# Half of the output projection computed inside the attention stage, and the prompt's compressed attention placed in its first steps

## What is computed

```python
q, g, cmp_r, sel_r, win_r, u = project(xp, norm1_g[l], w_in[l], ...)
o, win_state = nsa_prompt(q, g, cmp_r, sel_r, win_r, ...)      # sample: nsa_sample
y_pool, pool_state = pool_mix(u, ...)
...
def finish(x, o_attn, y_pool, w_out, norm2_g, peer_wq, ...):
    mix = jnp.concatenate([o_attn.reshape(B, T, ATTN_WIDTH), y_pool], axis=-1)
    h = x + jnp.einsum('btc,cd->btd', mix, w_out)
    return h + peer_ffn(rmsnorm(h, norm2_g), peer_wq, ...)
```

## Time and profile before

| | us |
|---|---|
| median of three runs | 1728.66 (1724.99 to 1734.77) |
| the profiled execution's own time | 1730.21 |
| its span | 1728.5 |
| `attend`, first matmul to the end of the last, in the trace | 146.3 to 351.5 |
| output projection, eight tiles | 353.8 to 404.6 |

### The profile page before, as it was taken

One profiled execution on the slowest core, in us unless ns is written; L12 is line 12 of the kernel. 1 busy time (PEld: TensorE's weight loads), 2 busy tenths in 40 slices (PEclk: granted clock), 3 DMA queues, 4 the chain that ended last, 5 costly groups with the idle time before them and its releaser, 6 DMA issues.

```text
span 1728.5 us, 29474 instructions
## 1 busy us (share of the span) xinstructions
PE 1669.6 (97%) x10320; PEld 1577.6 (91%) x10320; DVE 1368.2 (79%) x2811; ACT 736.4 (43%) x1391; POOL 495.2 (29%) x454
## 2 busy tenths in 40 slices
PE   8998998899998999999999999989999999999999
PEld 6876765589998999999999999989999999999999
DVE  3273457654788999999998998856998999999996
ACT  1121355443223334665666668833333333333332
POOL 0003232011000233333322244332443454444440
PEclk9999988899999999999999999989999999999999
DMA  7527242123222798888898999998999999999994
GB/s 223 185 62 219 74 122 76 38 86 99 78 68 92 259 320 306 292 317 310 305 319 305 314 327 373 377 346 282 373 390 377 365 396 393 391 395 398 393 394 143
DMA packets 188646, 457.31 MB, mean 265 GB/s; under 512 B 25858, under 2 KB 93954, under 8 KB 188034
## 3 DMA queue, kind: packets, MB, share of 16 engines
q1 hardware_dynamic: 111922, 245.27, 40.4%
q0 software_dynamic: 50416, 182.63, 28.8%
q10 hardware_dynamic: 26160, 27.53, 4.6%
HBM read 402.71 MB, written 56.05 MB: 265 GB/s over the span
## 4 chain that ended last, share of the span: by engine, by line
PE 61%; DVE 4%; DMA 2%; issue 1%; ACT 0%; SPq 0%; DVEq 0%; ACTq 0%
PE ps L1994 9%; PE ps L1997 9%; PE ps L2000 9%; PE ps L1970 9%; PE ps L1966 9%; PE ps L1967 9%; PE ps L2016 5%; DVE sb_w_lo L1799 1%; DMA gates_dense<-sb_g_stage 1%; DMA sb_ring<-expert_v 1%; DVE sb_slot L1836 0%; DMA sb_ring<-expert_u 0%; DVE sb_rows_y L1929 0%; DVE sb_hot L1835 0%; ACT sb_w_hi L1703 0%
## 5 line engine op out<-in xcount | busy, mean ns | idle before, releaser
L1703 ACT ACTIVATE sb_w_hi<-sb_ring 128x1024 fp32r<-128x1024 f32 x256 | 271.6, 1061 | 521.6 <-PE ps L2000 219.0
L1799 DVE TENSOR_TENSOR sb_w_lo<-sb_ring,sb_w_hi 128x1024 fp32r<-128x1024 f32 x256 | 313.0, 1223 | 74.8 <-ACT sb_w_hi L1703 68.2
L1966 PE MATMUL ps<-sb_x_hi,sb_w_hi 128*128 128x384 f32 x1024 | 353.4, 345 | 11.6 <-ACT sb_scores L1717 7.2
L1967 PE MATMUL ps<-sb_x_lo,sb_w_hi 128*128 128x384 f32 x1024 | 348.4, 340 | 0.0
L1970 PE MATMUL ps<-sb_x_hi,sb_w_lo 128*128 128x384 f32 x1024 | 202.6, 339 | 4.5 <-DVE sb_w_lo L1799 4.5
L1966 PEld LDWEIGHTS ps<-sb_x_hi,sb_w_hi 128*128 128x128 f32 x1024 | 194.4, 190 | 12.2 <-ACT sb_w_hi L1703 12.2
L1994 PE MATMUL ps<-sb_x_lo,sb_w_hi 128*128 128x384 f32 x1016 | 198.1, 336 | 5.4 <-ACT sb_x_lo L1712 5.3
L2000 PE MATMUL ps<-sb_x_lo,sb_w_hi 128*128 128x384 f32 x1016 | 197.6, 336 | 0.0
L1997 PE MATMUL ps<-sb_x_lo,sb_w_lo 128*128 128x384 f32 x1016 | 197.6, 336 | 0.0
L1967 PEld LDWEIGHTS ps<-sb_x_lo,sb_w_hi 128*128 128x128 f32 x1024 | 194.8, 190 | 0.0
L1693 POOL DMA_INDIRECT sb_scores<-expert_u_rows,sb_row_expert x80 | 103.5, 1293 | 307.2 <-DVE sb_row_dots L1918 216.0
(11 more groups left out here) (332 smaller groups left out, 2521.2 us busy)
## 6 DMA issues: line engine op xcount, KB each, us to landing
sb_ring<-expert_u SPq DMA_DIRECT2D x128, 512.0 KB
sb_ring<-expert_v SPq DMA_DIRECT2D x128, 512.0 KB
gates_dense<-sb_g_stage ACTq DMA_DIRECT2D x12, 2048.0 KB
hid_dense<-sb_hid SPq DMA_DIRECT2D x112, 192.0 KB
sb_scores<-hid_dense SPq DMA_DIRECT2D x112, 192.0 KB
sb_g_stage<-gates_dense SPq DMA_DIRECT2D x32, 384.0 KB
sb_g_stage<-gates_dense SPq DMA_DIRECT2D x48, 256.0 KB
sb_ring<-peer_wq SPq DMA_DIRECT2D x16, 512.0 KB
```

The source lines that it names most:

```text
L1703: nc.scalar.activation(whi[v % 2][:, :], ring(v)[:, :], ACT.Copy).then_inc(w_hi, 1)
L1799: nc.vector.tensor_tensor(wlo[v % 2][:, :], ring(v)[:, :], whi[v % 2][:, :], ALU.subtract).then_inc(w_lo, 1)
L1966: nc.tensor.matmul(out, hi[:, c * P:(c + 1) * P], g.x_hi[:, c], start=(c == 0), stop=False)
L1967: nc.tensor.matmul(out, hi[:, c * P:(c + 1) * P], g.x_lo[:, c], start=False, stop=False)
```

## The change

1. **Pooled half.** In steps 12 to 27, one piece n per step, PE computes the contribution of chunks 4 to 7 (pooling) to half n % 2 of the columns of output tile n // 2: four plain fp32 matmuls of 128x272 into bank 5 (`pooled`). DVE then adds the result to `g.xT` in place. Piece n waits until the add of piece n - 1 is made.
2. **Output projection.** `product` runs over four chunks instead of eight for the eight output tiles, so 24 matmuls instead of 48; high and low part are made of 512 columns of each `w_out` tile, and the split of `mixT` is of four chunks instead of eight. The query projection is unchanged.
3. **Compressed attention.** `cmp_scores` at steps 0, 2, 5, 8 instead of 0, 3, 11, 19; weights at 0, 3, 6, 9; transposes at 1, 4, 7, 10. All four pieces are in bank 5 before piece 0 of the pooled half, which waits for the last of them.
4. **Loads.** The pooled halves of `w_out` come in four loads of 2 tiles x 512 columns (512 KB), on SP's queue in `attend`: the first behind the page loads, the others behind `kv_mm` 2 and behind pieces 3 and 7; the attention halves follow as 256 KB each. The load of `w_out[0]` at the end of `project` and the 512 KB loads of the output stage go. The sample rows' buffers `h0[0]` and `h0[1]` trade ring places.

```diff
-        h0 = [g.ring[1 - e][:, :].rearrange("p (k b n) -> p k b n", k=4, b=EB) for e in range(2)]
+        h0 = [g.ring[e][:, :].rearrange("p (k b n) -> p k b n", k=4, b=EB) for e in range(2)]
...
+        pooled_mm, pooled_added = map(sem, ("pooled_mm", "pooled_added"))
+        pooled_w = lambda n: (g.ring[2 if n % 2 == 0 else 0][:, :], g.ring_in[2 if n % 2 == 0 else 0], 16 * (RING_OUT // 3 + 1 + n // 2 + n % 2))
...
-        cmp_at = {("mm", max(8 * j - 5, 0)): j for j in range(GRP)}
-        cmp_at.update({("weigh", max(8 * j - 4, 0)): j for j in range(GRP)})
-        cmp_at.update({("turn", max(8 * j - 3, 1)): j for j in range(GRP)})
+        cmp_at = {("mm", s): j for j, s in enumerate((0, 2, 5, 8))}
+        cmp_at.update({("weigh", s): j for j, s in enumerate((0, 3, 6, 9))})
+        cmp_at.update({("turn", s): j for j, s in enumerate((1, 4, 7, 10))})
+        POOLED = {s: n for n, s in enumerate(range(12, 12 + 2 * KC))}
...
+            def load_pooled(n):
+                w, done, _ = pooled_w(n)
+                sp.dma_start(w.rearrange("p (m n) -> p m n", m=2), g.a["w_out"][2 * n:2 * n + 2, :, D // 2:D].rearrange("m p n -> p m n")).then_inc(done, 16)
...
+            load_pooled(0)
...
                 if bt:
+                    sp.wait_ge(pooled_mm, 4)
+                    load_pooled(2)
+                    sp.wait_ge(pooled_mm, 8)
+                    load_pooled(3)
                     sp.wait_ge(so_mm, 1)
...
+                if bt == 0:
+                    sp.wait_ge(kv_mm, 2)
+                    load_pooled(1)
+            for t, n in ((RING_OUT, 12), (RING_OUT + 1, 16)):
+                sp.wait_ge(pooled_mm, n)
+                sp.dma_start(g.ring[t % 3][:, 0:D // 2], g.a["w_out"][t - RING_OUT][:, 0:D // 2]).then_inc(g.ring_in[t % 3], 16)
...
+            def pooled(n):
+                m, h = n // 2, n % 2
+                w, done, count = pooled_w(m // 2)
+                pe.wait_ge(done, count)
+                if n:
+                    pe.wait_ge(pooled_added, n)
+                else:
+                    pe.wait_ge(c_out, GRP)
+                for k in range(KC // 2):
+                    at = m % 2 * (D // 2) + k * P
+                    last = nc.tensor.matmul(bank(g, 5)[:, 0:HALF], w[:, at:at + P], g.mixT[:, KC // 2 + k, h * HALF:(h + 1) * HALF], start=(k == 0), stop=(k == KC // 2 - 1))
+                last.then_inc(pooled_mm, 1)
...
                 sub_pieces(s, 0)
+                if s in POOLED:
+                    pooled(POOLED[s])
...
+                if s in POOLED:
+                    n = POOLED[s]
+                    x = halves(g.xT[:, n // 2])[:, n % 2]
+                    dve.wait_ge(pooled_mm, n + 1)
+                    nc.vector.tensor_tensor(x, x, bank(g, 5)[:, 0:HALF], ALU.add).then_inc(pooled_added, 1)
...
+                kc = KH if c < KC else KC
...
-                for k in range(KC):
+                for k in range(kc):
...
-                nc.vector.tensor_tensor(wlo[c % 2][:, :], g.ring[(RING_OUT + c) % 3][:, :], whi[c % 2][:, :], ALU.subtract).then_inc(lo_made, 1)
+                n = KH * P if c < KC else KC * P
+                nc.vector.tensor_tensor(wlo[c % 2][:, 0:n], g.ring[(RING_OUT + c) % 3][:, 0:n], whi[c % 2][:, 0:n], ALU.subtract).then_inc(lo_made, 1)
...
-            for k in range(KC):
+            for k in range(KH):
                 nc.scalar.activation(mix[0][:, k], g.mixT[:, k], ACT.Copy).then_inc(hi_split, 1)
```

More of the change, by code:

```diff
@@ L115, with loaded @@
     pass
+def loaded(g, t):
+    twice = 2 if t >= RING_OUT and t % 3 != 1 else 0
+    return g.ring_in[t % 3], 16 * (t // 3 + 1 + twice)
 def halves(x):
@@ L1213, in output_and_queries @@
         NQ = 2 * PH
+        KH = KC // 2
         with ExitStack() as first:
-            mix = [memory(nc, first)[0](f"mix_{n}", [P, KC, T], F32R) for n in ("hi", "lo")]
+            mix = [memory(nc, first)[0](f"mix_{n}", [P, KH, T], F32R) for n in ("hi", "lo")]
         keys = sb("sub_keys", [P, NQ, NKEY])
@@ L1242, in _ @@
             sp.dma_start(norm2[:, :], g.a["norm2"]).then_inc(n_in, 16)
-            for t in range(RING_OUT + 2, RING_U + 3):
-                if t >= RING_OUT + 3:
-                    sp.wait_ge(lo_made, t - 3 - RING_OUT + 1)
+            for t in range(RING_OUT + 3, RING_U + 3):
+                sp.wait_ge(lo_made, t - 3 - RING_OUT + 1)
                 if t < RING_Q:
-                    w = g.a["w_out"][t - RING_OUT]
+                    sp.dma_start(g.ring[t % 3][:, 0:D // 2], g.a["w_out"][t - RING_OUT][:, 0:D // 2]).then_inc(g.ring_in[t % 3], 16)
+                    continue
                 elif t < RING_U:
@@ L1278, in product @@
                 pe.wait_ge(lo_made, c + 1)
-                for k in range(KC):
+                for k in range(kc):
                     for h in range(2):
-                        last = nc.tensor.matmul(at(h), lo[:, k * P:(k + 1) * P], x[0][:, k, half(h)], start=False, stop=(k == KC - 1))
+                        last = nc.tensor.matmul(at(h), lo[:, k * P:(k + 1) * P], x[0][:, k, half(h)], start=False, stop=(k == kc - 1))
                 last.then_inc(tile_mm, 1)
@@ L1300, in project @@
                     pe.wait_ge(h_added, KC - 1 + i)
-                product(KC + i, hg, 0 if i else KC + 1)
+                product(KC + i, hg, 0 if i else KH + 1)
             def score(i):
@@ L1436, in high_part @@
                 t = RING_OUT + c
-                act.wait_ge(g.ring_in[t % 3], 16 * (t // 3) + 16)
+                act.wait_ge(*loaded(g, t))
                 if c >= 2:
                     act.wait_ge(tile_mm, c - 1)
-                nc.scalar.activation(whi[c % 2][:, :], g.ring[t % 3][:, :], ACT.Copy).then_inc(hi_made, 1)
+                n = KH * P if c < KC else KC * P
+                nc.scalar.activation(whi[c % 2][:, 0:n], g.ring[t % 3][:, 0:n], ACT.Copy).then_inc(hi_made, 1)
             high_part(0)
-            for k in range(KC):
+            for k in range(KH):
                 nc.scalar.activation(mix[0][:, k], g.mixT[:, k], ACT.Copy).then_inc(hi_split, 1)
@@ L1699, in prepare_weights @@
             def prepare_weights(v):
-                act.wait_ge(*loaded(v))
+                act.wait_ge(*loaded(g, RING_U + v))
                 if v >= 2:
```

16 lines of the change are left out of this document (7 added, 9 removed).

## The result

The changed kernel takes 1716.45 us at the median (1709.50 to 1721.92), the kernel before 1726.09 in the same comparison: a ratio of 0.994, 95% interval 0.9925 to 0.9953. So it is faster by 0.6%; 1719.0 had been forecast, within 1711 to 1731. The profiled execution lies near the low end: 1710.29 us, span 1708.6, where that of before was 1730.21 and 1728.5 and lay above its median. So the two traces differ by twice what the medians do, and the stages tell more than the spans.

The account below looks back on a forecast made before the run. PE, busy for 97% of the span, was taken as the bound, with DVE at places in attention. Terms -21.5 + 1.4 + 10.7 - 0.5 = -9.9 from 1730.21 gave 1720.3, median-adjusted to 1718.8, rounded to 1719.0 us; range 1711 to 1731.

Parts of the forecast that it names:

- output projection: Eight output tiles with four chunks instead of eight: 3.3 us per tile instead of 6.00, in sum -21.5 us.
- steps 1 to 11: Two compressed attention pieces move to steps 5 and 8, step 11 gets shorter: +1.4 us (0 to +3).
- steps 12 to 27: Pooled pieces added: 82.6 us of work, 5.2 of holes, 2.5 of low clock, so +10.7 us (+4 to +18).
- steps 28 to 31: Work as before; one low stretch of 6.8 us may shrink: -0.5 us (-3 to +1).
- Rival D: One more low stretch and 9 us holes in steps 12 to 27, or output tiles at 3.8; 1723 to 1731; chance 0.25.
- rival C: Steps 12 to 27: waits for the single bank keep the grant at 0.81; about 1737 us; chance 0.10.
- rival B: Pooled pieces fill every hole, DVE keeps up, clock 1.00 from step 11 to 31; 1709 to 1714 us; chance 0.17.
- (1): Output projection: a tile takes 3.1 to 3.4 us, PE's short idle ended by ACT's high part.
- (2): `output_and_queries` begins about 12 us later than 352.
- (3): Steps 5 to 10 are 4 us longer.
- (4): 244 to 324 becomes about 90 us, grant above 0.9; DVE's add ends holes ahead of pooled matmuls, largest in step 17.
- (5): Each pooled piece in steps 12 to 27 takes 1.88 us.

Follow-up runs that it names:

- the short and the delayed add: Changed kernel, GpSimd's square add in the output projection over 8 of 544 columns (1708.97 us), or held back until DVE's low part is done (1712.54 us).
- parted scores: Changed kernel with the two halves of each compressed score piece on PE parted by the step's own scores: 1717.43 us, a single run.
- two edits: Changed kernel with GpSimd's square add held back behind DVE's low part and the compressed score halves parted: 1713.24 us, ratio 0.992.

## Why the prediction was right, and where it wasn't

The time was right to 2.6 us, partly because errors cancelled. Its terms, forecast and measured: output projection -21.5, -19.4; steps 1 to 11 +1.4, +4.25; steps 12 to 27 +10.7, +6.7; steps 28 to 31 -0.5, -4.0. The sum, -9.9, became -12.4 in the traces up to the query projection; a start of step 1 that was 1.1 us later makes it -11.3. The medians give -9.6. So the change itself was forecast to 0.3 us, and the 2.6 us are the kernel before, whose median was 1728.66 in three runs and is 1726.09 in twenty.

**The output projection: the tile was mis-sized.** "From the rows of one tile: low part 1.67 for 1024 columns, so about 0.84 for 512" is the step that failed. The earlier trace rows showed 1.22 and 1.67 for the same shape, and I halved the longer one. What made it long doesn't halve: it is the rest of GpSimd's add, as the short and the delayed add show. Undisturbed 512 columns take 0.69, beside GpSimd 1.55. The tiles with it take 4.06 and those without 3.0 to 3.1, so six periods from the second tile to the eighth take 22.39 (366.46 to 388.85) in place of 19.8. The first tile was 4.53 (4.47 by the sum), the last with the transition 4.43 (5.0 by the sum). The first tile had some luck: before, it held a low stretch, and so it does in nine of the eleven variants, where it takes 4.9 to 5.5. Rival D had the case, an output loop at 3.8 "because DVE's operations stretch where they crowd", with the size nearly right and the cause not: crowding on DVE does nothing, GpSimd does.

**Steps 1 to 11.** A compressed piece cost 2.0 us, as worked out: steps 1 to 10 grew by 7.8, less the 3.4 of two low stretches is 4.4 for the two pieces (4.2 forecast). Step 11 fell from 7.85 to 4.30, by 3.5 in place of 2.8. What I left out is that the new bursts of small matmuls can bring a low stretch with PE fully busy. That varies between runs, 0 or 3.4 us, and the range for this term (0 to +3) was too short by it.

**Steps 12 to 27.** The work was right: 82.50 us busy against 82.6. The holes were 3.8 us (5.2 forecast), all ended by DVE's add, the two largest in steps 16 and 17 as said. The low stretch priced at 2.5 didn't come in this trace. It did in five of the ten traces with all sixteen pieces in these steps, with a mean grant of 0.98. Ahead of the hole of step 17 it cost nothing (86.4 with the square add delayed): PE only came later to a DVE that was late anyway. Behind that hole it cost 1.7 (88.0 with parted scores, and with two edits).

**Steps 28 to 31.** "One low stretch of 6.8 us may shrink": it went altogether, worth 4.0, in the direction and beyond the bound (-3) that I gave.

**The clock rule.** The mechanism of rival C, that handing one PSUM bank back and forth brings short idles and thereby the low level, fell: the bank changes hands sixteen times, and the grant is 1.00 from step 11 to step 31 (0.98 in steps 12 to 27 of five other traces), against 0.82 with only the compressed attention moved. The Trainium skill's "A second HAM failure mode: psum-queue depth-cycling" (TensorE: Matmul & The Clock Gate), by which short idles at the cycling through PSUM banks make the clock swing, is not borne out at this place, where a single bank changes hands. Its "Loop structure matters more than you think", by which dense matmuls keep the clock up, is. My own sum had given the clock too little: in steps 11 to 31 the full level was worth about 6.7 us more than it held (0.7 in step 11, 2.5 in steps 12 to 27, 3.5 in steps 28 to 31), and rival B (0.17) described the attention better than the forecast did.

**The loads** were hidden, as forecast: no wait of PE in steps 12 to 27 ends on a DMA.

The list of signs: (1) the idle is ended by ACT's high part, as said, the tile is 4.06 and not 3.1 to 3.4; (2) PE enters the output projection 8.1 us later (353.81 to 361.93), not 12, since steps 12 to 31 were cheaper; (3) held, once the low stretches are taken off; (4) held but for the length, 86.3 and not 90; (5) held: a piece takes 1.9 (the pooled matmuls of step 16 start at 270.70, the transposes behind them at 272.61). One sum was off: the three low stretches of steps 12 to 27 are 30.6 us together, not 30.8, and nothing hangs on it.

## What to carry to other kernels

Ask what fills a stretch in which an engine waits and the clock is low: dense matmuls put there are paid at a fraction (11.3 of 30.0 us here, and 1.1 of 5.6 at the busiest place of DVE), and a piece moved to where PE has few such waits costs its full price. Before an operation's time is scaled with its size, look at what lies beside it; when two rows of the same shape differ, find the neighbour that makes the difference, as that part does not scale with the operation. Where two engines get in each other's way, moving one of them beside an operation that doesn't mind is a cheap cure (4.06 to 3.47 us per tile). And where a hole has one named releaser, test whether its place or the engine's load is the cause: moving it may mostly change who is seen waiting.

## What the runs showed of the hardware

- A DVE subtraction with both inputs in SBUF took 0.69 us for 512 columns alone and 1.55 beside a GpSimd add of 544 columns that had begun first; an add of 544 columns with an input in PSUM took 0.71 beside the same GpSimd add. That add took 1.35 to 1.37 alone or beside the latter, and 1.47 where it began 0.27 us before the end of a DVE operation with both inputs in SBUF.
- Low-clock stretches of 3.4 us came and went from run to run with the same code, in steps 1 to 10 right behind bursts of small matmuls (64 rows against 31 columns) and with PE busy 100%: both or neither, in four and five of nine traces. Each cost 1.7 us.
- Sixteen blocks of four dense fp32 matmuls raised the mean grant of steps 12 to 27 from 0.82 to 1.00 (0.98 in five of ten traces); with one matmul in each block it was 0.89.
